# Expert rows gathered beside the layer work of the next token tile, with native fp32 products

## The chip, the cores and the metric

One core of one Trainium2 chip runs the whole program. The metric is device time in microseconds of one execution, lower is better.

## What is computed

A block with mLSTM, attention and a gated feed-forward part comes first. Then two layers of a second model follow, each over 256 tokens of width 1024 in float32. Layer 0 has a convolution and pooling mixer, layer 1 a sparse attention beside an HGRN recurrence; both then do cross attention to 256 memory tokens and a PEER feed-forward part. The reference, cut to what matters here:

```python
for l in range(2):
    hn = rmsnorm(h, mix_norm[l])
    h = h + (short_conv_pool_mixer(hn, ...) if l % 2 == 0 else sparse_attn_hgrn_mixer(hn, ...))
    h = h + memory_cross_attn(rmsnorm(h, xattn_norm[l]), mem_n, ...)
    h = h + peer_ffn(rmsnorm(h, peer_norm[l]), peer_wq[l], peer_keys[l], peer_u[l], peer_v[l])
return rmsnorm(h, final_norm)

# peer_ffn, for each token: 8 heads, two sets of 128 keys
s1, i1 = top_k(s[:, :, 0], 16); s2, i2 = top_k(s[:, :, 1], 16)
top, pos = top_k(s1[..., :, None] + s2[..., None, :], 16)      # of 256 candidates
eid = i1 * 128 + i2 at pos                                     # 128 experts of 16384 per token
act = gelu(einsum('td,ted->te', x, u[eid]))
out = einsum('te,ted->td', softmax(top) * act, v[eid])
```

## The kernel before

256 tokens are two tiles of 128 (NT = 2), one token a partition. The arrays uv0 and uv1 hold a row of u and one of v side by side, 8 KB per expert. For a tile and j = 0..127 (SEL), POOL issues one indirect DMA that fetches expert j of each of the 128 tokens: 1 MiB, called a row of the ring here. The ring has 9 slots (RING).

Each engine runs its own program in order and waits on semaphores; nothing but the code's order decides what comes first.

- Dense products use weight tiles of 1024 x 512 (2 MB, four parts; a ring of six parts, loaded by SP). Outside the memory keys and values of layer 1, ACT rounds each part to fp32r (`high`, L1136), POOL subtracts to get the rest (`low`, L579), and PE multiplies three pairs, hi x hi, lo x hi and hi x lo (`product`, L714), for all 256 tokens: tokens as moving operand in blocks of 256 (`transposed`) or weights as moving operand, 512 wide (`natural`).
- Layer work goes stage by stage for both tiles: `odd` (layer 1 only), then cross attention, then the queries. A list unit on DVE (`top_lists`, `candidates`, `top_heads`, `keys_of`) finds the experts of two heads of one tile; four make a tile's 128. They run for tile 0 before the gathers; for tile 1 in pieces between the dots of tile 0.
- The expert rows of a layer follow, 2 x 128. POOL waits for a slot (`rows_done`) and issues (L636). DVE makes the product with the token's activation, held in two PSUM banks (`dots`, L2027), four rows at a time (GROUP). ACT takes the gelu (L1185), DVE multiplies by the gate (L2037), ACT makes a diagonal matrix per row (L1191), and PE adds diagonal x v row to two banks (L800), two products of 512 columns a row. In layer 0, tile 0, PE also makes memory keys and values of layer 1 between the groups, in native float32 (`memory`).
- PSUM banks are handed out by a plan (`make_plan`) in the order of fills.

Of the kernel before, what the change touches and what calls it, by code (L numbers as in the profile page):

```python
# [32 lines left out]
P = 128  # L33
S = 256
# [25 lines left out]
RING = 9  # L60
GROUP = 4
GROUPS = SEL // GROUP
DIAGS = 8

# [99 lines left out]

def make_plan():
# [32 lines left out]
    for l in range(2):  # L198
        if l:
            p.add("T7", 4)  # L200

            p.add("o_ckv")
            p.add("o_ik")
            p.add("o_hf", 2, "scalar")
            p.add("o_hi", 2)
            p.add("o_hg", 2)
            p.add("o_hq", 2)
            p.add("o_iq", 2)
            p.add("o_ql", 4)
            p.add("o_cT")  # L210
            p.add("o_kT", 2)
            p.add("h_d0", 2, "scalar")
            for n, h in enumerate(LEVELS):
                if n + 1 < len(LEVELS):
                    p.add(f"h_d{n + 1}", 2, "scalar")
                p.add(f"h_s{n}", 1 if h == P else NT)
            p.add("h_diag", NT)
            p.add("h_pv", NT)
            p.add("idx", 8, "scalar")
            units_of(p, "o", 8)  # L220
            p.add("o_pv", 4)
            p.add("lat_T", 4)
            p.add("o_yc", NT)
            p.add("o_yT", 4)
            p.add("o_out", 4)
        p.add(f"T{5 + 3 * l}", 4)
        p.add(f"x_q{l}", 4)
        units_of(p, f"x{l}", 4)
        p.add(f"x_pv{l}", 4)
        p.add(f"x_oT{l}", 4)  # L230
        p.add(f"x_o{l}", 4)
        p.add(f"T{6 + 3 * l}", 4)

        for n in range(PH // 2):
            p.add(f"p_q{l}{n}", 2, taker="scalar")
            p.add(f"p_s{l}{n}")
            p.add(f"p_r{l}{n}", taker="scalar")
        p.add(f"p_h{l}", 2, marks=0, hold=True)
        for t in range(NT):
            p.add(f"p_v{l}{t}", 2, marks=0, hold=True)  # L240
            if l == 0 and t == 0:
                p.add("x_k1", 4)
                p.add("x_v1", 4)
            if t == NT - 1:
                p.release(f"p_h{l}")
            p.release(f"p_v{l}{t}")
# [3 lines left out]
def tiles_in_order():  # L250
# [9 lines left out]
    for l in range(2):  # L260
# [6 lines left out]
        if l == 0:  # L267
            t += [("x_k1", 1), ("x_k1", 3), ("x_v1", 1), ("x_v1", 3)]
# [8 lines left out]
def build(nc, io):  # L277
# [6 lines left out]
    with ExitStack() as ctx:  # L284
# [261 lines left out]
        def _(po):  # L546
# [93 lines left out]
            def low_cross(layer):  # L640
# [5 lines left out]
                if layer == 0:  # L646
                    load_gain(7)
# [1577 lines left out]
```

## Time and profile before

| what | value |
|---|---|
| median of 3 runs | 2677.15 us (2676.20 to 2685.51) |
| the profiled execution | 2676.58 us, span 2674.3 us |
| mean granted clock of PE | 0.909 |
| PE, DVE, POOL, ACT busy | 2111.0, 1453.6, 1141.1, 653.1 us |
| moved by DMA | 735.58 MB, mean 275 GB/s |

### The profile page before, as it was taken

The page shows a single profiled execution, that of the slowest core. Times are in us where ns is not written, and L with a number is a line of the kernel's source. Part 1 is how long each engine was busy: PE and PEld are TensorE (multiplying, and loading weights), DVE is VectorE, ACT ScalarE, POOL GpSimd, SP SyncE. Part 2 cuts the span into 40 slices and gives each one's busy share as a digit, 9 for nine tenths or more (in the row PEclk, how much of TensorE's full clock was granted, in tenths as well). Part 3 has the DMA queues.
Part 4 walks back from the last instruction along what each step waited for, and adds up shares of the span by engine and source line. Part 5 has one row for each costly group of instructions (what it writes and reads, how often), then busy time and mean ns, then how long its engine had stood idle before and what let it go on. Part 6 is the DMA issues. An engine that isn't in the chain of part 4 may idle for free. (4 is left out here: it accounts for less than half of the span.)

```text
span 2674.3 us, 23831 instructions
## 1 busy us (share of the span) xinstructions
PE 2111.0 (79%) x8566; PEld 1373.4 (51%) x8566; DVE 1453.6 (54%) x3135; ACT 653.1 (24%) x1247; POOL 1141.1 (43%) x809
## 2 busy tenths in 40 slices
PE   3899989999688498887778768858775887878776
PEld 3755679888577344333333337847672333333332
DVE  6353232147535977755555545672388776455554
ACT  1322333443233111111111124233331111111111
POOL 2612457797536333332333338214362333333332
PEclk7898989999898799999999989979898989989988
DMA  8455445565324599999999956113337999999996
GB/s 318 144 174 166 168 145 171 167 193 176 118 94 144 229 424 425 422 419 389 393 426 426 426 223 194 62 52 114 102 136 320 426 425 426 421 379 426 426 423 291
DMA packets 126934, 735.58 MB, mean 275 GB/s; under 512 B 14264, under 2 KB 14264, under 8 KB 60512
## 3 DMA queue, kind: packets, MB, share of 16 engines
q0 software_dynamic: 77600, 555.18, 49.9%
q1 hardware_dynamic: 49072, 178.83, 20.5%
q8 instruction: 68, 1.11, 0.2%
q14 instruction: 50, 0.41, 0.0%
q10 hardware_dynamic: 144, 0.05, 0.0%
HBM read 732.94 MB, written 1.06 MB: 274 GB/s over the span
## 5 line engine op out<-in xcount | busy, mean ns | idle before, releaser
L579 POOL TENSOR_TENSOR W_lo<-W,W_hi 128x1024 fp32r<-128x1024 f32 x264 | 642.6, 2442 | 423.7 <-ACT W_hi L1136 423.0
L800 PE MATMUL banks<-arena 128*128 128x512 f32 x912 | 449.5, 642 | 150.4 <-ACT arena L1191 150.4
L800 PE MATMUL banks<-rows_b,arena 128*128 128x512 f32 x684 | 341.1, 646 | 122.0 <-ACT arena L1191 122.0
L1136 ACT ACTIVATE W_hi<-W 128x1024 fp32r<-128x1024 f32 x264 | 277.4, 1058 | 471.3 <-PE banks L714 389.0
L800 PEld LDWEIGHTS banks<-arena 128*128 128x128 f32 x912 | 182.0, 204 | 405.3 <-issue 259.2
L2027 DVE SCALAR_TENSOR_TENSOR arena<-arena,banks 128x1024 f32<-128x1024 f32 x228 | 276.3, 1220 | 193.3 <-DMA arena<-in_uv,p_eid 192.1
L636 POOL DMA_INDIRECT arena<-in_uv,p_eid x228 | 214.8, 942 | 385.0 <-PE banks L800 376.4
L714 PE MATMUL banks<-HT_hi,W_hi 128*128 128x256 f32 x1128 | 327.2, 290 | 35.2 <-DVE HT_lo L1576 13.4
L714 PE MATMUL banks<-HT_hi,W_lo 128*128 128x256 f32 x1128 | 324.8, 288 | 0.0
L714 PE MATMUL banks<-HT_lo,W_hi 128*128 128x256 f32 x1128 | 324.6, 288 | 0.0
L800 PEld LDWEIGHTS banks<-rows_b,arena 128*128 128x128 f32 x684 | 138.7, 208 | 317.7 <-issue 206.9
L636 POOL DMA_INDIRECT rows_b<-in_uv,p_eid x171 | 160.6, 939 | 307.6 <-PE banks L800 295.9
L2027 DVE SCALAR_TENSOR_TENSOR rows_b<-rows_b,banks 128x1024 f32<-128x1024 f32 x171 | 207.6, 1220 | 153.8 <-DMA rows_b<-in_uv,p_eid 151.4
L1185 ACT ACTIVATE arena<-arena 128x4 f32<-128x4 f32 x128 | 26.3, 205 | 1050.8 <-DVE arena L2031 1050.8
L800 PE MATMUL banks<-rows_c,arena 128*128 128x512 f32 x452 | 219.3, 625 | 47.8 <-ACT arena L1191 47.8
L714 PEld LDWEIGHTS banks<-HT_hi,W_hi 128*128 128x128 f32 x1128 | 222.9, 198 | 38.1 <-DVE HT_lo L1576 13.5
L714 PEld LDWEIGHTS banks<-HT_hi,W_lo 128*128 128x128 f32 x1128 | 222.7, 197 | 0.0
L714 PEld LDWEIGHTS banks<-HT_lo,W_hi 128*128 128x128 f32 x1128 | 222.3, 197 | 0.0
L2027 DVE SCALAR_TENSOR_TENSOR rows_c<-rows_c,banks 128x1024 f32<-128x1024 f32 x113 | 137.2, 1220 | 100.0 <-DMA rows_c<-in_uv,p_eid 99.5
L714 PE MATMUL banks<-W_hi,HT_hi 128*128 128x512 f32 (+1 forms) x400 | 159.8, 400 | 36.9 <-issue 16.6
L636 POOL DMA_INDIRECT rows_c<-in_uv,p_eid x113 | 106.3, 941 | 162.1 <-PE banks L800 160.0
L800 PEld LDWEIGHTS banks<-rows_c,arena 128*128 128x128 f32 x452 | 87.6, 198 | 170.8 <-issue 102.1
(260 smaller groups left out, 2641.4 us busy)
## 6 DMA issues: line engine op xcount, KB each, us to landing
W<-in_weights SPq DMA_DIRECT2D x336, 512.0 KB, 3.6
gain<-in_rows POOLq DMA_DIRECT2D x10, 512.0 KB, 5.9
arena<-in_uv,p_eid POOLq DMA_INDIRECT x228
rows_b<-in_uv,p_eid POOLq DMA_INDIRECT x171
arena<-in_rows POOLq DMA_DIRECT2D x1, 2048.0 KB, 17.0
arena<-in_keys POOLq DMA_DIRECT2D x2, 1024.0 KB, 5.0
arena<-bias_scratch POOLq DMA_DIRECT2D x2, 1024.0 KB, 7.7
rows_c<-in_uv,p_eid POOLq DMA_INDIRECT x113, 10.9
```

The source lines that it names most:

```text
L579: po.tensor_tensor(W_lo[:, slot, :], W[:, (PARTS * n + part) % RAW_RING, :], W_hi[:, slot, :].bitcast(F32), ALU.subtract).then_inc(S_("lo_ ...
L636: po.indirect_dma_start(rows[slot], None, table, bass.IndirectOffsetOnAxis(ap=p_eid[:, t, j:j + 1], axis=0))\
L714: mm = pe.matmul(bank[:, out], x if stationary else y, y if stationary else x, start=start, stop=last)
L800: mm = pe.matmul(sums[c], diag[:, n % DIAGS, :], rows[slot][:, D + c * BLK:D + (c + 1) * BLK], start=j == 0, stop=j == SEL - 1)
L1136: act.activation(W_hi[:, q % SPLIT_RING, :], wait_landed(act, n, part), ACT.Copy).then_inc(S_("hi_made"), 1)
L1185: act.activation(a, a, ACT.Gelu_apprx_tanh).then_inc(S_("gelu_ready"), 1)
L2027: v.scalar_tensor_tensor(out=u, in0=u, scalar=1.0, in1=h, op0=ALU.mult, op1=ALU.mult, accum_out=p_act[:, t, j:j + 1]).then_inc(S_("row_dot ...
```

## The change

From the end of the even output on, the program is cut into four chains, (layer 0, tile 0), (layer 0, tile 1), (layer 1, tile 0), (layer 1, tile 1). A chain does one tile's layer work: `odd` if in layer 1, `cross`, `queries`. In chains 1 to 3, places (`feed`) are written into the code of DVE, ACT and PE; at each, the engine does its share of the next pair of rows (GROUP = 2) of the chain before. PE's place k does pair k - 2 (LAG). What is left of a chain's 64 pairs after its places is done at its end (`drain`). There are 39 places in `odd`, 15 in `cross`, 10 in `queries` and 16 in `memory`, which now follows the queries of chain 1. The last chain's rows are drained alone.

Dense products in the chains are native float32, 128 tokens at a time, straight from the parts that SP loads; ACT and POOL don't split them, and each weight tile of a layer is loaded once per token tile. POOL only issues gathers there. The dot's second operand is H in SBUF. The gelu is 0.5 a g (1 + tanh(...)): DVE makes two small products and a third, ACT a Tanh and one Identity a row. Gains, keys, masks and bias windows come from SP (`tables`), in its order among the weight parts, behind waits. The ring has 8 slots. The last norm, too, goes tile by tile.

```diff
-RING = 9
-GROUP = 4
+RING = 8
+GROUP = 2
+LAG = 2
...
+CHAINS = [(l, t) for l in range(2) for t in range(2)]
...
+            def tables(stage, i):
...
+                elif stage == "o_ik.3":
+                    load_masks(3)
...
+                elif i == 0 and stage in ("o_ql.2", "o_ql.3"):
+                    c = int(stage[-1])
+                    sp.wait_ge(S_("scratch_written"), 16)
+                    sp.wait_ge(S_("hscores_ready"), c - 1)
...
@@ PE
+            def weigh(g):
+
+                c = at[0]
+                for j in range(g * GROUP, (g + 1) * GROUP):
+                    n, slot, turn = row_of(c, j)
                     pe.wait_ge(S_("diag_ready"), n + 1)
...
+                    for b in range(2):
+                        mm = pe.matmul(banks[:, plan.bank(f"p_v{c}", b), :], diag[:, n % DIAGS, :],
+                                       rows[slot][:, D + b * BLK:D + (b + 1) * BLK], start=j == 0, stop=j == SEL - 1)
                     mm.then_inc(rows_done, 1)
...
+            def feed():
+
+                if at[0] is not None:
+                    if LAG <= at[1] < GROUPS + LAG:
+                        weigh(at[1] - LAG)
+                    at[1] += 1
+
+            def drain():
+
+                for g in range(max(at[1] - LAG, 0), GROUPS):
+                    weigh(g)
+                at[0] = None
+
+            def dense(stage, i, blocks):
+
+                n = tile_no[stage] + i
+                bank = claim(stage, i)
+                for part in range(PARTS):
+                    w = raw(n, part)
+                    for b, (out, columns, stationary) in enumerate(blocks):
+                        for j in range(2):
+                            x, y = w[:, j, columns], HT[:, 2 * part + j, :]
+                            mm = pe.matmul(bank[:, out], x if stationary else y, y if stationary else x,
...
+                    if part % 2:
+                        feed()
...
+            def queries(c, l, t):
+
+                turn_norm(c, 6 + 3 * l, t)
                 for n in range(PH // 2):
...
+                    dense(f"p_q{n}.{c}", 0, blocks4)
...
+            for c, (l, t) in enumerate(CHAINS):
+                if c:
+                    begin(c - 1)
+                if l:
+                    odd(c, t)
+                cross(c, l, t)
+                queries(c, l, t)
+                if c == 1:
+                    memory()
+                if c:
+                    drain()
+            begin(3)
+            drain()
...
@@ ACT
+            def row_weights(g):
+
+                c = at[0]
+                e = slice(g * GROUP, (g + 1) * GROUP)
+                act.wait_ge(S_("dots_ready"), c * GROUPS + g + 1)
+                step(act.activation(p_tanh[:, e], p_poly[:, e], ACT.Tanh, scale=0.7978845608028654))
                 for j in range(g * GROUP, (g + 1) * GROUP):
...
+                    step(act.activation(p_w[:, j:j + 1], p_tanh[:, j:j + 1], ACT.Identity, scale=p_half[:, j:j + 1],
+                                        bias=p_half[:, j:j + 1]))
...
@@ DVE
+            def dots(g):
...
+                    v.scalar_tensor_tensor(out=u, in0=u, scalar=1.0, in1=H[:, t, :], op0=ALU.mult, op1=ALU.mult,
+                                           accum_out=p_act[:, j:j + 1]).then_inc(S_("row_dots"), 1)
...
+                step.overlap(v.scalar_tensor_tensor(out=p_half[:, e], in0=a, scalar=0.5, in1=p_g[:, t, e], op0=ALU.mult,
+                                                    op1=ALU.mult))
+                stt(p_poly[:, e], a, 0.044715, a, ALU.mult, ALU.mult)
+                stt(p_poly[:, e], p_poly[:, e], 1.0, a, ALU.add, ALU.mult, "dots_ready")
...
+            def queries(c, l, t):
+
+                norm1(c, 6 + 3 * l, t)
+                feed(4)
+                for n in range(PH // 2):
+                    after(v, f"p_s{n}.{c}")
+                    top_lists(l, n)
+                    if n < PH // 2 - 1:
+                        feed()
+                    candidates(l, 2 * n, 2 * n + 2)
+                    top_heads(l, 2 * n, 2 * n + 2)
+                    keys_of(l, t, 2 * n, 2 * n + 2)
+                    if n < PH // 2 - 1:
+                        feed()
+                if c == 1:
+                    feed(16)
```

How the order moves on PE, at the output product of the cross attention of layer 1. Before (L788 sums with the values, L733 transposes, L714 the three products of the split operands, which then repeat):

```order
L1074 MATMUL banks<-x_kT,arena 128x256 x4
L778 MATMUL banks<-const,arena 128x128 x12
L788 MATMUL banks<-arena 128x256 x16
L733 MATMUL banks<-const,H 128x128 x16
L714 MATMUL banks<-W_hi,HT_hi 128x512
L714 MATMUL banks<-W_lo,HT_hi 128x512
L714 MATMUL banks<-W_hi,HT_lo 128x512
```

The same place of chain 2 in the change (L846 is `weigh`, L878 `dense`, L893 the transposes):

```order
L1206 MATMUL banks<-arena 128x256 x8
L846 MATMUL banks<-rows_b,arena 128x512 x4
L893 MATMUL banks<-const,H 128x128 x8
L846 MATMUL banks<-rows_c,arena 128x512 x4
L878 MATMUL banks<-W,arena 128x512 x4
L846 MATMUL banks<-arena 128x512 x4
L878 MATMUL banks<-W,arena 128x512 x4
L846 MATMUL banks<-arena 128x512 x2
L846 MATMUL banks<-rows_b,arena 128x512 x2
```

The dense work of one tile is native, and four products of the rows before stand after every half weight tile and every hand-over.

On DVE, at a list unit. Before, tile 0 (L2052 takes the scores, L1953 to L1971 make the lists, L1408 the candidates, then the heads):

```order
L2052 COPY arena<-banks 128x512
L1953 MAX arena<-arena 128x8 x4
L1955 MAX_INDEX p_idx<-arena 128x8 x4
L1957 MATCH_REPLACE arena<-arena 128x128 x4
L1959 MAX arena<-arena 128x8 x4
L1961 MAX_INDEX p_idx<-arena 128x8 x4
L1971 CAST arena<-p_idx 128x64
L1408 TENSOR_TENSOR arena<-arena 128x512
L1953 MAX arena<-arena 128x8 x2
```

In chain 1 of the change (L2098 is the dot, L2103 and L1672 the small products behind it):

```order
L2284 MAX arena<-arena 128x8 x4
L2286 MAX_INDEX p_idx<-arena 128x8 x4
L2288 MATCH_REPLACE arena<-arena 128x128 x4
L2290 MAX arena<-arena 128x8 x4
L2292 MAX_INDEX p_idx<-arena 128x8 x4
L2300 CAST arena<-p_idx 128x64
L2098 SCALAR_TENSOR_TENSOR rows_c,arena<-rows_c,H 128x1024 x2
L2103 SCALAR_TENSOR_TENSOR arena<-arena 128x2
L1672 SCALAR_TENSOR_TENSOR arena<-arena 128x2 x2
L1666 TENSOR_TENSOR arena<-arena 128x512
L2284 MAX arena<-arena 128x8 x2
```

The copy of the scores is gone (ACT takes them), and a pair of dots stands between the lists and the candidates.

## Rows read from the trace of the kernel before

**Rows 1.** The page, 40 slices: DMA engines busy in tenths, and GB/s.
```profile
DMA  8455445565324599999999956113337999999996
GB/s 318 144 174 166 168 145 171 167 193 176 118 94 144 229 424 425 422 419 389 393 426 426 426 223 194 62 52 114 102 136 320 426 425 426 421 379 426 426 423 291
```

**Rows 2.** Stages: us; busy of PE, PEld, DVE, ACT, POOL; PEclk, DMA share, GB/s.
```profile
0.00:732.10 732.10, 617.95 (x3356) 514.04 (x3356) 311.41 (x455) 242.78 (x291) 406.10 (x183) 0.91 0.54 176
732.10:816.00 83.90, 69.21 (x400) 61.06 (x400) 27.00 (x50) 32.07 (x49) 38.57 (x17) 0.94 0.36 113
816.00:915.00 99.00, 59.64 (x464) 58.27 (x464) 76.98 (x267) 27.13 (x36) 44.35 (x26) 0.80 0.53 187
915.00:1582.00 667.00, 540.31 (x1216) 238.57 (x1216) 394.89 (x898) 101.42 (x328) 232.61 (x248) 0.94 0.96 401
1582.00:1838.40 256.40, 193.97 (x1242) 176.15 (x1242) 145.54 (x247) 89.53 (x132) 105.37 (x49) 0.89 0.32 102
1838.40:1922.10 83.70, 68.96 (x400) 60.91 (x400) 27.00 (x50) 30.79 (x48) 38.61 (x18) 0.94 0.36 113
1922.10:2020.50 98.40, 59.56 (x464) 58.18 (x464) 77.20 (x266) 27.13 (x36) 43.41 (x25) 0.80 0.41 151
2020.50:2653.70 633.20, 494.26 (x1008) 203.26 (x1008) 387.05 (x884) 98.44 (x321) 232.03 (x247) 0.91 0.98 409
2653.70:2674.30 20.60, 7.13 (x16) 2.96 (x16) 6.50 (x22) 3.78 (x9) 0.00 (x0) 0.77 0.13 51
```

**Rows 3.** DVE in the gathers, timeline: start, us, engine, line, operation [idle before <-releaser].
```profile
1385.19 0.16 DVE L2037 TENSOR_TENSOR arena<-arena 128x4 f32<-128x4 f32 x1 [0.27 <-ACT arena L1185]
...
1388.35 1.22 DVE L2027 SCALAR_TENSOR_TENSOR arena<-arena,banks 128x1024 f32<-128x1024 f32 x1 [1.20 <-DMA arena<-in_uv,p_eid]
```

**Rows 4.** Timelines of PE and its weight loads: list scores, memory part, expert rows.
```profile
842.35 2.02 PE L1097 MATMUL banks<-arena 128*128 128x128 f32 x16 [0.79 <-issue]
...
1021.45 3.62 PE L714 MATMUL banks<-arena,W 128*128 128x256 f32 x16
...
1409.26 0.19 PEld L800 LDWEIGHTS banks<-rows_b,arena 128*128 128x128 f32 x1 [0.24 <-issue]
```

**Rows 5.** Timeline of ACT: the four diagonals of a group.
```profile
1414.79 1.28 ACT L1191 ACTIVATE arena<-const,arena 128x128 f32<-128x128 f32 x4 [0.23 <-DVE arena L2037]
```

**Rows 6.** Timeline of DVE: first tile's halves of the even output.
```profile
719.12 0.69 DVE L1526 TENSOR_TENSOR X<-banks,X 128x512 f32<-128x512 f32 x1 [12.74 <-PE banks L714]
...
730.00 0.69 DVE L1526 TENSOR_TENSOR X<-banks,X 128x512 f32<-128x512 f32 x1 [8.83 <-PE banks L714]
```

**Rows 7.** Timeline of DVE: a list with POOL splitting, and one (910.18) without.
```profile
865.26 0.69 DVE L2052 COPY arena<-banks 128x512 f32<-128x512 f32 x1
...
877.45 3.49 DVE L1998 TENSOR_TENSOR arena<-arena 128x512 f32<-128x512 f32 x2
...
882.83 0.69 DVE L2052 COPY arena<-banks 128x512 f32<-128x512 f32 x1
...
910.18 1.29 DVE L1998 TENSOR_TENSOR arena<-arena 128x512 f32<-128x512 f32 x2
```

**Rows 8.** Timeline of the last norm, ACT and DVE.
```profile
2662.04 1.06 ACT L1154 ACTIVATE H<-X 128x1024 f32<-128x1024 f32 x1 [6.34 <-PE banks L800]
...
2664.90 0.17 DVE L1411 TENSOR_SCALAR st<-st 128x2 f32<-128x2 f32 x1 [1.38 <-ACT H L1154]
...
2667.27 2.60 DVE L1414 SCALAR_TENSOR_TENSOR H<-X,st,gain 128x1024 f32<-128x1024 f32 x2
```

**Rows 9.** Timeline of DVE: an HGRN level's products (three such) and masked scores.
```profile
1716.97 1.22 DVE L1408 TENSOR_TENSOR arena<-arena 128x1024 f32<-128x1024 f32 x1
1718.23 1.29 DVE L1893 TENSOR_TENSOR arena<-banks,arena 128x512 f32<-128x512 f32 x2
```

**Rows 10.** Stage table as in group 2: gathers, memory tiles, lists together.
```profile
936.00:1137.00 201.00, 176.43 (x453) 86.98 (x451) 145.29 (x392) 28.18 (x95) 73.02 (x78) 0.97 1.01 424
```

**Rows 11.** Gather issues on POOL, line 636: duration ns min/median/max, first and last start.
```profile
L636 POOL DMA_INDIRECT arena<-in_uv,p_eid x228: 932/936/1389, 885.4 to 2630.7; - x114
```

More of the change, by code:

```diff
@@ L197, in make_plan @@
     p.add("e_out", 4)
[L198 to L246, printed above, removed]
+    for c, (l, t) in enumerate(CHAINS):
+        chain(p, c, l, t)
+        if c:
+            p.release(f"p_v{c - 1}")
+        p.add(f"p_v{c}", 2, marks=0, hold=True)
+    p.release("p_v3")
     return p
@@ new lines, in _ @@
+            for c, (l, t) in enumerate(CHAINS):
+                if c:
+                    at[:] = [c - 1, 0]
+                if l:
+                    odd(c, t)
+                cross(c, l, t)
+                queries(c, l, t)
+                if c == 1:
+                    memory()
+                act.wait_ge(S_("top_ready"), c + 1)
+                step(act.activation(p_g[:, t, :], p_g[:, t, :], ACT.Exp), "top_exp")
+                if c:
+                    drain()
+            at[:] = [3, 0]
@@ L1403, in _ @@
+            after(act, "p_v2", 1)
+            squares(0)
+            drain()
+            after(act, "p_v3", 1)
+            squares(1)
         @block.vector
@@ new lines, in feed, with drain @@
+            def feed(n=1):
+                for _ in range(n):
+                    if at[0] is not None and at[1] < GROUPS:
+                        dots(at[1])
+                        at[1] += 1
+            def drain():
+                c = at[0]
+                l, t = CHAINS[c]
+                for g in range(at[1], GROUPS):
+                    dots(g)
+                at[0] = None
+                v.wait_ge(rows_done, (c + 1) * SEL)
+                for b in range(2):
+                    xs = X[:, t, b * BLK:(b + 1) * BLK]
+                    step.free(v.tensor_tensor(xs, banks[:, plan.bank(f"p_v{c}", b), :], xs, ALU.add), f"p_v{c}", b)
@@ L2101, in _ @@
-            norm(10, X, gain_of(10), signal="final_ready")
+            for c, (l, t) in enumerate(CHAINS):
+                if c:
+                    at[:] = [c - 1, 0]
+                if l:
+                    odd(c, t)
+                cross(c, l, t)
+                queries(c, l, t)
+                softmax_top(c, t)
+                if c:
+                    drain()
+            at[:] = [3, 0]
+            norm1(3, 10, 0, "final_ready")
+            drain()
+            norm1(3, 10, 1, "final_ready")
```

1219 lines of the change are left out of this document (675 added, 544 removed).

## The prediction

> **What bounds the kernel now.** I read the slices of the span first, to find which resource is full where [rows 1]: the DMA engines stand at 9 tenths or more in two stretches, about 15 slices, and at 1 to 6 tenths over most of the rest. The stage table [rows 2] names them. From 915 to 1582 us and from 2020.5 to 2653.7 us the expert rows of a layer come in, 256 rows of 1 MiB, at 401 and 409 GB/s; the layers' other stages move 102 to 187 GB/s while PE is busy 69 of 84 us, 60 of 99, 194 of 256. So the kernel alternates: 1300 us bound by the gathers, 621 us of layer work (84 + 99 + 256 + 84 + 98) in which DMA mostly idles, and 732 us of front that the change leaves alone. In the gathers, DVE waits 1.20 us for each row beside 1.22 us of work [rows 3]. By bytes a row costs 1.05 MB / 426 GB/s = 2.46 us, a weight tile of 2.1 MB costs 4.92 us.
>
> **The change, part by part.** The program becomes four chains (layer, token tile); the rows of one chain are handled inside the next one's work, a pair per place. Prices of a place:
> - *DMA*: a pair is 4.92 us; there are 64 a chain.
> - *PE*: a row is 4 records of 0.43 us (a load of 0.19 and 0.24 of idle) [rows 4], so a pair is 3.44 us.
> - *DVE*: two products of 1.22 and three small operations of 0.16 with their waits, 3.1 us [rows 3].
> - *ACT*: before, four diagonals take 1.28 us [rows 5]; two of them, a Tanh and two small Identity are about 1.5 us. Never the bound.
>
> *Native fp32.* Before, a weight tile serves 256 tokens in 10.9 us (the second halves of the even output land at 719.12 and 730.00) [rows 6]. Native with 512 columns it is 16 records of 0.43 = 6.9 us for 128 tokens. With 128 columns it is 64 records; 16 of them take 2.02 us [rows 4], which would be 8.1, but a quarter of 0.43 is 0.108, and the row's last end is modelled, so 7 us. Two token tiles now cost 14 instead of 10.9. Their weights are read twice, 26 tiles x 4.92 = 128 us of DMA more, inside idle DMA time if the interleaving works. The splitting on ACT and POOL goes. That matters to DVE: its two 512-wide products of the key lookup take 3.49 us beside POOL's subtractions and 1.29 us where POOL only issues gathers [rows 7].
>
> *Chain 0* (no rows beside it). Cross attention: 4 tiles = 28 us, and for one tile instead of two the remaining 39 of the 84 us shrink to some 29 (a norm is 1.06 on ACT, 2.4 for the root and 1.3 for the product on DVE [rows 8], and halving the tokens doesn't halve the hand-overs): 57. Queries: norm, transposes and first tile 18 us, then four lists on DVE. One list took 17.6 us (from 865.26 to 882.83) [rows 7]; less the 2.2 of the stall, the copy of 0.7 that goes to ACT and some small stalls it is 14.2, so 57; with the softmax 78. Together 135, against 183 now (84 + 99).
>
> *Cross with rows* (15 places). PE: 15 x 3.44 + 28 + 12 for transposes, scores and sums = 92. DMA: 15 x 4.92 + 4 x 4.92 = 94. These are nearly equal, and the start (norm, first place without a pair, as PE lags by two) is exposed: 108.
>
> *Queries with rows* (10 places). DVE is the bound: 27 us to the first list, then 3 x (14.2 + 2 x 3.1) + 14.2 = 75, softmax 2: 105. DMA would need 69, so 36 us of it are lost in each of three chains.
>
> *Memory keys and values* (chain 1). PE 16 x (3.4 + 3.44) = 110: 16 records of 256 columns in 3.62 us are one such part [rows 4]. DMA needs 98. I take 114.
>
> *Rest of chain 1's rows*: 64 - 15 - 10 - 16 = 23 places at the pace of DMA, 113. With 6 us of hand-over (last sums, add) chain 1 is 108 + 105 + 114 + 113 + 6 = 446.
>
> *Odd mixer* (39 places, 10 weight tiles, one smaller). PE: 134 + 66 + 33 = 233. DMA: 39 x 4.92 + 49 + 10 for tables (a table of 1 MiB is 2.46) = 251. The HGRN levels are paced by DVE: half of 3 x 1.22 + 1.29 and 3.1, with waits about 5.9 a level [rows 9], 8 us over DMA in all. With start and hand-overs 272 for the first tile, 282 for the second, whose keys are twice as many. SP now waits for events of the chain before it loads masks and bias windows, and the weights of the next tiles queue behind those waits (the latent queries' behind the HGRN scores); PE has its sums and the index scores to do meanwhile, so I cost it at 0, and at 5 us, two such tables, if that cover is too short. Chain 2 = 272 + 108 + 105 + 4 = 489, chain 3 = 499.
>
> *End*: 128 rows with 8 already there, 120 x 2.46 = 295, and 17 for the last pair, norm of one tile instead of two and half the output (20.6 now [rows 2]): 312.
>
> Sum: 732 + 135 + 446 + 489 + 499 + 312 = 2613 us of span. The profiled execution takes 2676.58 for a span of 2674.3, and the median is 0.6 above it, so **2615 us**, 62 less. Put differently, hiding 1300 us of gathers under layer work saves much less than that work lasts, because PE has 220 us of row work per chain and most layer work is PE's too.
>
> Why not much worse: one stretch of before already does this. From 936 to 1137 us rows, memory tiles and list pieces run together at 424 GB/s, PE 176 of 201 us busy at a granted clock of 0.97 [rows 10].
>
> A page speaks against the DMA terms. The trace holds 426 GB/s for slices on end [rows 1]. The Trainium skill (SBUF — State Buffer, Summary: rules for kernel authors) says to estimate HBM to SBUF with 358 GB/s; by it a row would cost 2.9 us and the last drain alone 351. The row decides.
>
> **The rivals.**
> 1. *Near the DMA floor.* If places hide hand-overs entirely, and lists run while 8 rows buffer, chains 1 to 3 cost their bytes: 374 + 413 + 418 and the queries' 36 each, with 25 for starts: 732 + 135 + 1338 + 312 = 2517. For: [rows 10]. Against: 8 slots hold 20 us, and lists leave longer gaps.
> 2. *Slower: the clock in the chains.* PE is in program order behind DVE and ACT at every place. Where it pauses, the granted clock falls: 0.80 in the query stages (busy 60%), 0.89 in the odd mixer (76%), 0.94 in cross (82%) [rows 2]. PE at 0.8 would need 291 for the odd mixer, 115 for cross, 138 for memory; with the 39, 16 and 4 us of idle that I allow kept beside it, that is 330, 131, 142: 2 x 58 + 3 x 23 + 28 = 213 more, 2828. These stages hold 2 x 233 + 3 x 92 + 110 = 852 us of PE at full clock, so the gain of 62 is gone at 852 / (852 + 62) = 0.93. For: hand-overs at 64 places. Against: the places fill just those pauses with PE work, DMA sets the pace in half of them and hides a slower PE there, and [rows 10] have 0.97.
>    The Trainium skill (TensorE: Matmul & The Clock Gate, HAM oscillation — how this bites in real kernels) describes bursts between waits that keep finding a slow clock; the rows on the query stages agree with it.
> 3. *The dots fight for a port.* The dot's second operand moves from the banks to H in SBUF, so both come from SBUF. An issue on POOL is 0.936 us at the median and 1.389 at most [rows 11]. If each dot waited one issue, a pair on DVE would be 5.0 us: lists 3 x 11, levels 2 x 15, other places 20, and 64 x 0.1 in each drain: 90 more, 2705. Bounds: 0 (the median issue is as short as the shortest, though DVE often works on two SBUF operands beside it) to 0.94.
>    The Trainium skill (SBUF — State Buffer, Who interferes with whom) states that a DVE instruction with two SBUF inputs contends with a GpSimd instruction that reads SBUF; by it this rival holds, as far as issuing reads the indices. The before trace has no such dot.
> 4. *Nothing in sum*: interleaving gains and native fp32's extra 3.1 us for 26 tiles (80 us) cancel: 2664 to 2690.
>
> **How the numbers follow.** Forecast (2560 to 2664): 0.50. Rival 1: 0.15. Rival 2: 0.19. Rival 3: 0.04. Rival 4: 0.12. A measurement tells 0.5%, 13 us, from no change; below 2664 is faster: 0.50 + 0.15 = 0.65; same 0.12; slower 0.19 + 0.04 = 0.23. The range takes rival 1 in and reaches into rival 2: 2515 to 2735. The forecast's own is 2560 to 2664.
>
> **What would show it.** First row issue near 820 us and first dots near 867. DMA at 0.9 or more in cross and odd stages, 0.6 to 0.7 in queries; the queries of chains 1 to 3 about 105 us with DVE over 80% busy; PE's clock there at 0.8, elsewhere at 0.95 or more; four dense tiles at 7 us each net. A final drain of 2.46 us a row. Wrong if: the dots last over 1.3 us (rival 3); PE's clock in the odd mixer is below 0.93 (rival 2); odd plus cross of one chain last over 420 us at full clock, which would mean ordering waits that I have not seen, a take on ACT stuck behind a pair that hasn't landed.

## The result and the profile after

The changed kernel takes 2557.74 us (median of 4 runs, 2555.51 to 2559.21) against 2680.7 us (4 runs, 2676.2 to 2685.51): a ratio of 0.954, 95% interval 0.9518 to 0.9562. It is 123 us faster where 62 were forecast. That is inside the range of 2515 to 2735, but 2 us below the band of the forecast's own theory (2560 to 2664), on the side of rival 1. The profiled execution has a span of 2555.4 us.

The page, 40 slices of some 64 us. They answer to the slices of before [rows 1]:

```profile
PE   3898979999688498798779999985999998587776
PEclk7999989998889698899989999997999999799999
DMA  8455445565336599699999999986999999399997
GB/s 321 146 173 186 140 165 165 173 189 182 124 132 230 202 418 410 248 382 424 425 364 422 400 424 409 404 337 253 421 399 405 418 402 414 141 407 425 425 425 298
```

Before, the DMA engines were full in two blocks, with some 440 us of little traffic between them. Now they are at 9 from the 18th slice on, but for the 27th and 28th (the queries of chain 2), the 35th (the end of those of chain 3) and the last. The stage table, cut at DVE's adds to X (and, at 861.0, where chain 0's lists are done), shows the same (us; busy of PE, PEld, DVE, ACT, POOL; PEclk, DMA share, GB/s; it answers to [rows 2]):

```profile
0.00:727.10 727.10, 610.56 (x3356) 508.24 (x3356) 311.26 (x455) 240.63 (x289) 402.39 (x181) 0.92 0.54 177
727.10:782.10 55.00, 43.81 (x216) 32.60 (x216) 8.04 (x24) 8.32 (x17) 0.00 (x0) 0.91 0.45 157
782.10:861.00 78.90, 38.63 (x296) 37.12 (x296) 59.93 (x260) 8.58 (x15) 7.96 (x8) 0.76 0.61 224
861.00:955.70 94.70, 87.55 (x324) 52.44 (x325) 49.94 (x126) 30.70 (x89) 27.60 (x26) 0.93 0.84 340
955.70:1289.60 333.90, 279.98 (x893) 151.24 (x891) 199.95 (x602) 93.90 (x269) 113.70 (x102) 0.95 0.94 380
1289.60:1539.90 250.30, 230.29 (x923) 134.29 (x924) 167.76 (x413) 90.94 (x252) 78.67 (x75) 0.97 0.98 402
1539.90:1642.20 102.30, 94.06 (x336) 54.85 (x335) 50.74 (x129) 32.84 (x94) 32.63 (x30) 0.93 0.99 403
1642.20:1754.70 112.50, 80.82 (x390) 54.33 (x388) 88.86 (x329) 24.34 (x66) 24.47 (x24) 0.88 0.78 309
1754.70:2008.10 253.40, 237.95 (x963) 142.94 (x963) 165.71 (x407) 92.85 (x251) 81.68 (x74) 0.97 0.98 397
2008.10:2109.00 100.90, 92.02 (x333) 53.52 (x332) 50.61 (x129) 32.66 (x93) 31.34 (x29) 0.95 1.00 407
2109.00:2221.80 112.80, 82.25 (x392) 55.15 (x390) 88.85 (x330) 24.20 (x66) 26.39 (x25) 0.88 0.77 307
2221.80:2547.50 325.70, 241.31 (x512) 94.53 (x512) 187.38 (x463) 108.06 (x323) 138.99 (x120) 0.97 0.93 388
```

In order the rows are front, cross attention and queries of chain 0, cross attention of chain 1, its queries with memory tiles and drain, then odd mixer, cross attention and queries of chain 2 and of chain 3, and the last drain. Three readings lead the rest. In the odd mixers and the cross attentions of chains 2 and 3 the DMA engines are 0.98 to 1.00 busy. In the queries they are at 0.77, and nothing else is full either: DVE 89 of 113 us, PE 82. And the last drain takes 325.7 us at a share of 0.93, though it has nothing to do but rows.

The forecast against the stages, in us:

| stage | forecast | measured | difference |
|---|---|---|---|
| front | 732 | 727.1 | -5 |
| chain 0: cross, queries | 57, 78 | 55.0, 78.9 | -1 |
| chain 1: cross | 108 | 94.7 | -13 |
| chain 1: queries, memory, drain | 338 | 333.9 | -4 |
| chain 2: odd mixer | 272 | 250.3 | -22 |
| chain 2: cross, queries | 108, 109 | 102.3, 112.5 | -2 |
| chain 3: odd mixer | 282 | 253.4 | -29 |
| chain 3: cross, queries | 108, 109 | 100.9, 112.8 | -3 |
| end | 312 | 333.6 | +22 |

### The profile page after: what moved, and what is told of

Its sections match the earlier page's. It is cut to its first block, busy times and chain, and to the rows that moved or that the text cites. A ratio compares the mean times of both kernels' runs of the same rounds, so it can differ in the third digit from the quotient of the medians.

```text
span 2555.4 us, 26072 instructions
## 1 busy us (share of the span) xinstructions
PE 2119.2 (83%) x8926; PEld 1371.3 (54%) x8926; DVE 1432.2 (56%) x3674; ACT 789.2 (31%) x1821; POOL 965.8 (38%) x693
## 4 chain that ended last, share of the span: by engine, by line
PE 48%; DVE 24%; DMA 19%; ACT 5%; issue 3%; POOL 1%; DVEq 0%; SPq 0%; ACTq 0%; POOLq 0%
PE banks L846 16%; PE banks L758 14%; DMA rows_b<-in_uv,p_eid 13%; PE banks L878 9%; DMA rows_c<-in_uv,p_eid 4%; DVE arena L1666 3%; PE banks L1028 2%; DVE rows_b L2098 2%; PE banks L915 2%; DVE arena L1672 2%; DMA W<-in_weights 2%; ACT arena L1333 1%; DVE rows_c L2098 1%; DVE arena L2098 1%; DVE arena L2288 1%
## 5 line engine op out<-in xcount | busy, mean ns | idle before, releaser
L714 POOL DMA_INDIRECT arena<-in_uv,p_eid x192 | 213.1, 1110 | 669.8 <-PE banks L846 557.9
L667 POOL TENSOR_TENSOR W_lo<-W,W_hi 128x1024 fp32r<-128x1024 f32 x160 | 392.8, 2461 | 189.4 <-ACT W_hi L1280 188.9
L846 PE MATMUL banks<-arena 128*128 128x512 f32 x768 | 362.5, 610 | 85.6 <-ACT arena L1339 85.6
L846 PE MATMUL banks<-rows_b,arena 128*128 128x512 f32 x768 | 363.9, 612 | 26.6 <-ACT arena L1339 26.6
L2098 DVE SCALAR_TENSOR_TENSOR rows_b<-rows_b,H 128x1024 f32<-128x1024 f32 x192 | 233.7, 1224 | 197.6 <-DMA rows_b<-in_uv,p_eid 196.6
L2098 DVE SCALAR_TENSOR_TENSOR arena<-arena,H 128x1024 f32<-128x1024 f32 x192 | 233.9, 1225 | 177.9 <-DMA arena<-in_uv,p_eid 175.7
L714 POOL DMA_INDIRECT rows_b<-in_uv,p_eid x192 | 209.6, 1092 | 324.2 <-PE banks L846 314.8
L846 PEld LDWEIGHTS banks<-arena 128*128 128x128 f32 x768 | 140.7, 193 | 260.2 <-issue 158.7
L878 PEld LDWEIGHTS banks<-arena,W 128*128 128x128 f32 x2080 | 254.0, 200 | 31.2 <-issue 18.2
L878 PE MATMUL banks<-arena,W 128*128 128x128 f32 x2080 | 257.8, 284 | 11.1 <-ACT arena L1361 6.5
L846 PE MATMUL banks<-rows_c,arena 128*128 128x512 f32 x512 | 235.4, 603 | 33.5 <-ACT arena L1339 33.5
L846 PEld LDWEIGHTS banks<-rows_b,arena 128*128 128x128 f32 x768 | 147.9, 198 | 211.5 <-issue 167.8
L714 POOL DMA_INDIRECT rows_c<-in_uv,p_eid x128 | 140.7, 1099 | 248.3 <-PE banks L846 244.6
L2098 DVE SCALAR_TENSOR_TENSOR rows_c<-rows_c,H 128x1024 f32<-128x1024 f32 x128 | 155.3, 1225 | 118.3 <-DMA rows_c<-in_uv,p_eid 117.4
L1333 ACT ACTIVATE arena<-arena 128x1 f32<-128x1 f32 x512 | 197.9, 387 | 17.4
L758 PE MATMUL banks<-HT_hi,W_hi 128*128 128x256 f32 x608 | 177.2, 291 | 22.9 <-DVE HT_lo L1834 13.4
L1339 ACT ACTIVATE arena<-const,arena 128x128 f32<-128x128 f32 x512 | 177.6, 394 | 8.3
L846 PEld LDWEIGHTS banks<-rows_c,arena 128*128 128x128 f32 x512 | 94.9, 192 | 152.3 <-issue 99.4
L758 PE MATMUL banks<-HT_hi,W_lo 128*128 128x256 f32 x608 | 176.2, 290 | 0.0
```

The lines of the kernel that those rows point to most:

```text
L667: po.tensor_tensor(W_lo[:, slot, :], W[:, (PARTS * n + part) % RAW_RING, :], W_hi[:, slot, :].bitcast(F32), ALU.subtract).then_inc(S_("lo_ ...
L714: po.indirect_dma_start(rows[slot], None, io[f"uv{l}"], bass.IndirectOffsetOnAxis(ap=p_eid[:, t, j:j + 1], axis=0))\
L758: mm = pe.matmul(bank[:, out], x if stationary else y, y if stationary else x, start=start, stop=last)
L846: mm = pe.matmul(banks[:, plan.bank(f"p_v{c}", b), :], diag[:, n % DIAGS, :], rows[slot][:, D + b * BLK:D + (b + 1) * BLK], start=j == 0, ...
L878: mm = pe.matmul(bank[:, out], x if stationary else y, y if stationary else x, start=part + b + j == 0, stop=part == PARTS - 1 and b == le ...
L1333: step(act.activation(p_w[:, j:j + 1], p_tanh[:, j:j + 1], ACT.Identity, scale=p_half[:, j:j + 1], bias=p_half[:, j:j + 1]))
```

## The experiments

All runs are edits of the changed kernel. e1, e4, e8, e9 and e10 ran once; the others are medians of 4 or 6 runs, and their ratios are to the kernel before on the same chip, whose median lay between 2682 and 2685 us there. A few us of a total come from the front, which no edit touches: in the profiled executions it took 727.1 to 732.0 us. A stage that an edit leaves alone differs by up to 4 us from one execution to another.

### What the overlap is worth: e1_no_places

```diff
             def feed():
-                if at[0] is not None:
-                    if LAG <= at[1] < GROUPS + LAG:
-                        weigh(at[1] - LAG)
-                    at[1] += 1
+                pass
```

(the same for ACT's and DVE's `feed`.)

> Every place in the layer code is empty on PE, ACT and DVE, so all 128 rows of a chain are handled in its drain, and nothing of the native fp32 products or of the tile-by-tile order changes. Theory A (the gain is the overlap; native fp32 and one token tile at a time cost time by themselves): front 727, chain 0 133, chain 1 57 + 78 + 55 of memory tiles + 120 x 2.46 + 6 = 491, chains 2 and 3 some 150 + 57 + 78 + 301 = 586 each, end 334: 2857 us of span, between 2780 and 2900. Rival B (the gain comes from dropping the splits and the stalls of DVE beside POOL, the places add little): 2600 to 2700, near the kernel before.

Measured: 2847.49 us, span 2845.7. Chain 2 without rows, and its drain:

```profile
1339.00:1468.70 129.70, 108.86 (x621) 84.00 (x621) 57.13 (x141) 29.09 (x59) 0.00 (x0) 0.88 0.55 196
1468.70:1523.70 55.00, 43.32 (x216) 32.11 (x216) 8.00 (x23) 8.18 (x18) 0.00 (x0) 0.91 0.53 181
1523.70:1602.00 78.30, 36.77 (x296) 35.44 (x296) 59.76 (x258) 7.43 (x13) 0.00 (x0) 0.76 0.26 82
1602.00:1921.90 319.90, 239.08 (x512) 93.55 (x512) 183.63 (x450) 106.92 (x321) 148.40 (x128) 0.98 1.01 424
```

Theory A holds: 583 us for chain 2 where it said 586. So the change is a loss of 171 us (2845.7 against 2674.3) and a gain of 290 (2845.7 against 2555.4). The loss sits where a token tile costs more than half of two: two cross attentions of 55 against 84, two lots of queries of 78 against 99 [rows 2], about 2 x (26 + 57) = 166 over both layers. In the queries this is mostly overlap that the kernel before had and e1 lacks: its 99 us hold the lists of tile 0 only, and those of tile 1 ran between the dots. The odd mixer costs 129.7 and 137.2 for two tiles against 256.4 before, 10 us more. That native fp32 and dropping the splits are by themselves the gain is refuted. What native fp32 costs apart from the order by token tile, no run separates.

### What sets the pace beside the rows: e4, e9, e10

```diff
-                    for b in range(2):
+                    for b in range(2 if j in (0, SEL - 1) else 1):
```

> PE leaves out the second half of the v sum for all rows of a chain but the first and the last: a pair costs PE 1.72 us and not 3.44. Theory A (DMA sets the pace of the odd mixer, of cross attention and of the drains, DVE that of the queries): no stage gets shorter by more than 5 us but the cross attention of chain 1; 2530 to 2557. Rival B (PE in program order sets the pace of the odd mixer): 39 x 1.72 = 67 us less in each odd mixer and up to 26 in each cross attention, 2350 to 2450.

Measured: 2548.78 us, span 2547.0, 8 less, and inside theory A's band. The odd mixer and cross attention of chain 2:

```profile
1282.00:1536.50 254.50, 190.31 (x775) 118.89 (x775) 167.70 (x413) 90.33 (x252) 84.24 (x76) 0.87 0.96 391
1536.50:1634.80 98.30, 72.90 (x276) 43.42 (x276) 50.75 (x129) 32.56 (x94) 32.03 (x30) 0.86 1.01 417
```

PE is busy 40 us less and its granted clock drops from 0.97 to 0.87, yet the odd mixer is no shorter (254.5 against 250.3). PE's time there, at either clock, was not what was paid for. The 8 us came from chain 1's queries, memory tiles and drain, 325.9 us where 333.9 stood; the cross attention of chain 1, which theory A let get shorter, did not (see the hand-overs below).

e9 takes bytes away instead. It leaves out three quarters of each weight part in chains 2 and 3:

```diff
+                width = PW // 4 if tiles[n][0][-2:] in (".2", ".3") else PW
-                sp.dma_start(W[:, m % RAW_RING, :], io["weights"][weight_no[n]][:, part * PW:(part + 1) * PW])\
+                sp.dma_start(W[:, m % RAW_RING, 0:width],
+                             io["weights"][weight_no[n]][:, part * PW:part * PW + width])\
```

> In chains 2 and 3 only the first quarter of each weight part is loaded, the products then read what the slot held before: 3.7 us of transfer less for each tile, 37 us in an odd mixer and 15 in a cross attention, with all of PE's work left. Theory A (DMA sets the pace there, and PE, 230 of 250 us busy, is close behind): PE takes over, an odd mixer gets 8 to 15 us shorter, a cross attention 4 to 8, the queries don't change: 2515 to 2535. Rival B (DMA's 0.98 is a coincidence, the order of the hand-overs sets the pace): no stage changes by more than 3 us, 2552 to 2560. Rival C (DMA alone counts, PE has room): 2 x (37 + 15) = 104 less, 2454.

> The thin weights of e9 and the half v sum of e4 together: PE's 1.72 us a row pair less as well, in all chains. Theory A (two limits that lie close together in the odd mixer, DMA at 251 and PE at 233 by the forecast): each alone gives little, both together much: an odd mixer goes to 214 to 228 us, a cross attention to 80 to 88, 2465 to 2500 in all, more than the sum of what e4 (9 us) and e9 give. Rival B (hand-overs): the sum of e4 and e9, no more.

Measured: e9 2510.94 us (span 2507.7), e10 2445.92 us (span 2444.1). Odd mixer and cross attention of chain 2, first of e9:

```profile
1290.00:1525.70 235.70, 222.71 (x912) 131.92 (x913) 167.03 (x414) 91.85 (x252) 82.11 (x72) 0.98 0.94 361
1525.70:1616.50 90.80, 89.70 (x339) 51.78 (x338) 50.81 (x129) 32.55 (x94) 34.46 (x30) 1.00 1.00 389
```

and of e10:

```profile
1274.00:1491.60 217.60, 177.29 (x775) 112.12 (x775) 167.38 (x413) 90.69 (x252) 83.00 (x76) 0.91 0.98 397
1491.60:1579.80 88.20, 70.38 (x276) 42.76 (x276) 50.53 (x128) 32.65 (x94) 32.51 (x30) 0.88 0.99 396
```

With fewer bytes (e9) the odd mixer loses 15 us and PE is 94% busy; the cross attention loses 11.5 and PE is 99% busy. With both edits the odd mixer goes to 217.6. The spans fall by 8 and 48 us apart and by 111 together, twice the sum. Two limits lie close together, DMA first and PE 15 us behind. Both edits keep every hand-over and the number of transfers. e9 came out 4 us under theory A's band, since a cross attention gave 10 to 12 us where it said 4 to 8; rival C (PE has room) and the hand-over rivals are refuted. These are single executions, but the effects on the stages, 10 us and more, are well over the 4 us of spread.

### How far PE may lag: e3 and e8

```diff
-LAG = 2
+LAG = 1
```

(e8: `LAG = 3`.)

> LAG = 1: PE adds a pair one place behind DVE and ACT. Theory A (odd mixer and cross attention are at the DMA engines' limit, 0.98 to 1.00 busy, so PE's hand-overs are hidden, and what an earlier sum gives is only that the first slots of a chain come free one place sooner): 0 to 15 us less, 2543 to 2558. Rival B (a lag of one makes PE wait for ACT's diagonals, 1 to 2 us, at most of the 39 + 15 + 10 places): 2600 or more, with PE idle before the row products for ACT, and a lower clock in the odd mixer.

> LAG = 3: PE adds a pair three places behind DVE and ACT, so 6 of the 8 slots hold rows that are already multiplied, and 2 are left in flight. Theory A (what matters of the lag is how many slots it leaves to the transfers; a row lands some 5 to 8 us after its issue, and DVE waits for it in front of layer work that PE waits for): the HGRN levels and other hand-overs get 3 to 6 us longer at each of some 20 places in an odd mixer and 6 in a cross attention: 2620 to 2750 us, DMA well under 0.98 in the odd mixer; the last drain is unchanged at 324 us. Rival B (a longer lag only takes PE off the wait for ACT): 2550 to 2560.

Measured: e3 2556.97 us (4 runs), ratio 0.9524 [0.9498, 0.955]; e8 2651.73 us, span 2648.3. Chain 2 of e3, odd mixer, cross attention, queries:

```profile
1295.30:1542.50 247.20, 230.32 (x920) 134.27 (x921) 166.93 (x413) 93.06 (x254) 78.53 (x74) 0.97 0.99 407
1542.50:1640.00 97.50, 90.53 (x339) 51.91 (x338) 50.85 (x129) 31.86 (x91) 35.78 (x30) 1.00 1.02 421
1640.00:1757.40 117.40, 84.17 (x390) 54.16 (x388) 88.68 (x329) 24.37 (x66) 26.35 (x24) 0.86 0.76 297
```

and of e8, with the last drain:

```profile
1302.30:1575.60 273.30, 235.63 (x917) 139.91 (x917) 167.65 (x413) 90.50 (x252) 80.04 (x74) 0.93 0.94 370
1575.60:1690.40 114.80, 96.20 (x336) 55.87 (x336) 50.75 (x129) 32.44 (x94) 31.18 (x30) 0.91 0.90 360
1690.40:1809.10 118.70, 83.98 (x392) 57.65 (x392) 88.77 (x329) 24.01 (x66) 26.39 (x24) 0.85 0.75 288
2316.00:2640.40 324.40, 239.09 (x512) 93.74 (x512) 187.35 (x463) 108.08 (x323) 138.75 (x120) 0.97 0.93 390
```

Against the table of the changed kernel, a lag of one gives 3 and 5 us in the odd mixer and cross attention and gives 5 back in the queries, all near the spread of a stage; the total, 2556.97, is unchanged and in theory A's band (2543 to 2558). I had not expected that loss. It is DVE's wait for the scores of the first list, in the changed kernel and in e3:

```profile
1669.92 0.88 DVE L2284 MAX8 arena<-arena 128x8 f32<-128x128 f32 x4 [4.13 <-ACT arena L1361]
1672.82 0.87 DVE L2284 MAX8 arena<-arena 128x8 f32<-128x128 f32 x4 [8.98 <-ACT arena L1361]
```

ACT's copy of the first query tile ahead of it waits 7.06 us for PE's dense products in e3 and 3.68 in the changed kernel. A lag of three costs 23, 12 and 6 us in one chain and nothing in the drain, which has no places; 2651.73 us is in theory A's band (2620 to 2750), and rival B said 2550 to 2560. DMA's share falls from 0.98 to 0.94 in the odd mixer, and DVE's longest wait for a row there grows from 2.5 to 5.8 us. That fits theory A, that the lag has to leave slots for transfers: 4 of 8 are enough, 2 are not. The number of slots was not changed by itself.

### The queries: e2_take_first

In the trace of the changed kernel DVE waits 2.4 us or more in front of the search of each of the four key lists of a chain with rows. ACT, ahead of list 3 in chain 3 (start, us, engine, line, operation, [idle before <-releaser]):

```profile
2202.05 0.20 ACT L1331 ACTIVATE arena<-arena 128x2 f32<-128x2 f32 x1 [9.77 <-DVE arena L1672]
2202.28 0.81 ACT L1333 ACTIVATE arena<-arena 128x1 f32<-128x1 f32 x2
2203.12 0.69 ACT L1339 ACTIVATE arena<-const,arena 128x128 f32<-128x128 f32 x2
2203.72 0.57 ACT L1361 ACTIVATE arena<-banks 128x512 f32<-128x512 f32 x1
```

and DVE, for which that last copy is the scores to search:

```profile
2204.39 0.90 DVE L2284 MAX8 arena<-arena 128x8 f32<-128x128 f32 x4 [2.44 <-ACT arena L1361]
```

PE had the scores ready, but ACT takes them behind its share of the pair, which DVE has only just multiplied. The edit swaps the two:

```diff
                     take(p_qT[l], f"p_q{n}.{c}")
-                    feed()
                     if n:
                         act.wait_ge(S_("lists_ready"), (PH // 2) * c + n)
                     take(p_s[l], f"p_s{n}.{c}")
+                    feed()
```

> ACT copies the key scores of list n before it works on the pair of that place, not behind it. Theory A (DVE sets the pace of the queries, and each of lists 1 to 3 waits 2.44 us for this copy): 3 x 2.44 less in three chains, 22 us, so about 2536 us and a ratio of 0.945 to 0.947; the queries of chains 2 and 3 take 105 us and no longer 113. Rival B (the queries wait for transfers or for PE, DVE's wait only moves): 2553 to 2560, as without the edit.

Measured: 2533.66 us, ratio 0.9445 [0.9418, 0.9472]. The queries of chain 2:

```profile
1636.10:1741.20 105.10, 79.55 (x390) 52.91 (x388) 88.71 (x330) 24.74 (x66) 27.17 (x25) 0.93 0.84 332
```

105.1 us where 112.5 stood, with DVE's work unchanged at 88.7, and the wait in front of lists 1 to 3 is gone. Theory A holds, with 24 us where it said 22 (the ratio is just under its 0.945 to 0.947); rival B said no change.

### The ends of chains: e5, e6, e7

```diff
             at[:] = [3, 0]
+            feed(8)
             norm1(3, 10, 0, "final_ready")
             drain()
```

(ACT likewise, ahead of `squares(0)`.)

> The last norm of token tile 0 comes after 8 pairs of the last drain, not ahead of them. Theory A (from the last list to the first new row issue DMA is empty, and DVE's norm of 4.9 us lies on that path; later in the drain DVE waits 2 us a pair and hides it): 5 us less, about 2553 us, ratio 0.951 to 0.953; the last drain from the add of chain 2 to that of chain 3 takes 319 us and no longer 324. Rival B (the first issues wait for something else, such as PE's sums or POOL): no change, 2556 to 2559.

Measured: 2553.37 us (6 runs), ratio 0.9524 [0.9497, 0.9551]. By the total alone 4 us are at the edge of what is told apart. By the stage they are plain: from the add at 2223.53 to that at 2544.22 us is 320.7 against 325.7. The empty stretch at the head of the drain, in the changed kernel on POOL:

```profile
2210.35 0.94 POOL L714 DMA_INDIRECT rows_c<-in_uv,p_eid  x1 [1.79 <-PE banks L846]
2235.35 0.94 POOL L714 DMA_INDIRECT arena<-in_uv,p_eid  x1 [24.07 <-PE banks L846]
```

and in e5:

```profile
2212.07 0.94 POOL L714 DMA_INDIRECT rows_c<-in_uv,p_eid  x1 [1.76 <-PE banks L846]
2231.99 0.94 POOL L714 DMA_INDIRECT arena<-in_uv,p_eid  x1 [18.99 <-PE banks L846]
```

In the changed kernel no row is asked for during 25.0 us: all 8 slots are taken, POOL waits until PE frees one, and PE until DVE has finished list 3, the softmax and the norm and has multiplied a pair. Without the norm it is 19.9 us.

e6 moves two places of the odd mixer into that stretch:

```diff
-                dense(f"o_hi.{c}", 0, wide)
+                dense(f"o_hi.{c}", 0, wide, places=False)
...
                     top_lists(l, n)
-                    if n < PH // 2 - 1:
-                        feed()
+                    feed()
...
                     keys_of(l, t, 2 * n, 2 * n + 2)
-                    if n < PH // 2 - 1:
-                        feed()
+                    feed()
```

(PE and ACT each get two places behind the loop over the lists, and ACT and DVE one `feed(2)` fewer beside o_hi; `places=False` leaves out the two of that product.)

> Two places of the odd mixer (beside its product o_hi) move behind the last list of the queries, in each chain with rows. Theory A (the odd mixer and the drain of chain 1 are at DMA's limit, 4.92 us a place; DVE sets the pace of the queries, 2.87 us a place, and DMA idles at their end): 3 x 2 x (4.92 - 2.87) = 12 us less, 2545 us, the queries 6 us longer and the odd mixers 10 us shorter. Rival B (PE or the hand-overs set the pace of the odd mixer, so that fewer places there give nothing): 17 us more, 2570 to 2580.

> The edits of e2, e5 and e6 together. Theory A (they act at three different places of the path): 24 + 5 + 12 = 41 us less, 2511 to 2523 us, ratio 0.937 to 0.941. Rival B (with e2 the queries are no longer DVE's alone, and the places moved there meet PE or DMA): 2525 to 2540.

Measured: e6 2563.98 us, ratio 0.9565 [0.9529, 0.96], 6 us slower; e7 2540.15 us, ratio 0.9475 [0.944, 0.9509], slower than e2 alone (2533.66). e6's 2563.98 fits neither of its theories; e7's is at the upper edge of rival B's band (2525 to 2540). The intervals of the ratios overlap those of the runs they are compared with, and 5 of e6's 6 us could be the front, which took 732.0 us in its profiled execution against 727.1. From the front's end to the last add e6 takes 1824.0 us against 1820.3. What is sure is that the 12 us that theory A promised did not come. Half of A came true: e6's odd mixers take 241.6 and 242.8 us, 9 and 11 less. But its queries take 126.1 and 123.4, 14 and 11 more and not 6. DVE's waits at the end of e6's chain 3 show why:

```profile
2225.36 0.29 DVE L2359 TENSOR_REDUCE st<-arena 128x8 f32<-128x128 f32 x1 [1.78 <-ACT arena L1652]
2230.05 1.42 DVE L2127 TENSOR_TENSOR X<-banks,X 128x512 f32<-128x512 f32 x2 [3.83 <-PE banks L846]
```

The last pair stands right before the end of the chain, so the softmax waits behind ACT's diagonals (0.50 before) and the add waits for PE's sum (no wait before). These two waits are 5.1 us more and the two pairs some 6, together the 11 of chain 3.

### The version that follows: e11 and e12

e11 is e2 and e5 together. e12 adds the places of e6, but puts the second one before `keys_of`, the last step of the last list unit, and not behind it:

```diff
                     top_heads(l, 2 * n, 2 * n + 2)
+                    if n == PH // 2 - 1:
+                        feed()
                     keys_of(l, t, 2 * n, 2 * n + 2)
```

> The edits of e2 and e5 together, without that of e6. Theory A (both lie on the path, at different places): 24 + 5 = 29 us less, 2525 to 2532 us, ratio 0.941 to 0.944. Rival B (one takes the other's place): 2533 or more.

> The edits of e11, and the two places that e6 moved, but the second one ahead of the last key list and not behind it. Theory A (what e6 paid over 5.7 us a chain is the softmax behind ACT's diagonals, 1.3 us, and the add behind PE's sum of the last pair, 3.8 us; with some 9 us of DVE work behind the pair both are hidden): 4 to 12 us less than e11, 2515 to 2524 us, and queries of 111 us in chains 2 and 3 where e7 had 116 to 118. Rival B (each place in the queries costs 5 to 6 us, wherever it stands): 2532 to 2542, as e7.

Measured: e11 2533.56 us (6 runs), ratio 0.9443 [0.9418, 0.9468]; e12 2522.14 us (6 runs), ratio 0.9399 [0.9374, 0.9423]. In e12 the same two operations read:

```profile
2188.03 0.29 DVE L2363 TENSOR_REDUCE st<-arena 128x8 f32<-128x128 f32 x1 [0.44 <-ACT arena L1652]
2188.91 1.42 DVE L2128 TENSOR_TENSOR X<-banks,X 128x512 f32<-128x512 f32 x2
```

At this place the second wait is gone and the first is 0.44 us (in chain 2 the add still waits 0.90). The queries take 113.1 and 110.9 us, and e12 is 11 us faster than e11: theory A. By its total, e11 falls into rival B's band (2533 or more) by 0.6 us, and its interval overlaps e2's. Its trace speaks for A: both edits do what they did alone (queries of 105.1 us, last drain 321.5), and from the front's end to the last add it takes 1791.3 us, the 29 less than 1820.3 that A said. e12 takes 1783.4. e12 is the fastest of the runs that leave nothing out, 36 us below the changed kernel.

## Why the prediction was right, and where it was off

**The mechanism** was right: the gathers run under layer work, DMA is full in odd mixer and cross attention, and drains run at the pace of rows. PE's sum for an odd mixer, 233 us, was measured at 230.3 and 238.0. The size of the gain was not: 123 us and not 62. Chains 1 to 3 came out 73 us under the forecast, front and chain 0 together 6 under, and the end 22 over it, so part of the error cancels in the 57 us by which the span is shorter.

DMA's sum, 251, was met by the stage itself, 250.3 and 253.4, but in part by luck. POOL issued 75 rows in the first odd mixer and not the 78 of 39 pairs, and the stage moved 402 GB/s x 250.3 us = 100.6 MB, which at 426 GB/s would take 236 us. Fewer bytes and a lower rate than assumed cancel.

**The terms that were too dear** are the hand-overs. The prediction put 21 us on top of DMA's 251 in the first odd mixer and 31 in the second ("with start and hand-overs 272 ... 282"), and 14 on top of 94 in each cross attention. Most of the missing gain lies there: 50 us came back in the two odd mixers, 26 in the three cross attentions. A stage that is at DMA's limit doesn't pay for its hand-overs as long as landed rows wait in slots, and the second tile's doubled keys are hidden as well. e4, e9 and e10 show this limit; e8 shows that two slots free for transfers are too few for it.

The cross attention of chain 1 is another case, and half of the 26 us are its. It consists of a start and a stretch at DMA's limit:

```profile
861.00:878.00 17.00, 9.97 (x45) 8.41 (x46) 13.80 (x39) 6.09 (x17) 0.00 (x0) 0.60 0.15 47
878.00:955.70 77.70, 77.58 (x280) 44.03 (x279) 36.14 (x87) 24.61 (x72) 27.60 (x26) 1.00 1.00 404
```

The start, 17 us in which all 8 slots are taken and none is free for an issue, was even longer than the 14 forecast. What was too dear is DMA's 94: 8 rows were there already, and POOL issued 26 in the stage and not 30. The stage moved 340 GB/s x 94.7 us = 32 MB, where 94 us at 426 GB/s are 40. In e4, with half of PE's row products gone, the two parts take 16.9 and 77.6 us.

**The queries** were sized well but for one wait: 105 and 4 forecast, 112.5 and 112.8 measured. The list of 14.2 us with 6.2 of pairs was right: the period is 22.4 us (from 2181.97 to 2204.39), of which 2.44 are ACT's late copy, and 20.0 are left. e2 took it away and got 105.1. The sentence "a take on ACT stuck behind a pair" stood among the signs, but for the odd mixer, where DMA set the pace; it should have been priced in the one stage where DVE sets the pace.

**The end** was 22 us too cheap. The rate was right: the issues from 2235.35 to 2526.5 us are 120 in 291.2, one every 2.45 us. But the first comes 13.5 us after the add, because 8 landed rows don't keep DMA busy, they block it until the first pair is summed; and from the last issue to the end 28.9 us pass, where I had 17.

**Native fp32** was right: 64 records of 128 columns take 7.31 us between 800.35 and 807.7, and in chain 0 two halves of an output follow each other in 6.87 us (the adds at 774.50 and 781.37). Front and chain 0 came within 6 us in all, and the ordering waits on SP show no cost: DMA is 0.98 busy in the stages that have them.

**The rivals.** Rival 1 (2517), which I gave a chance of 0.15, was nearer than my own forecast: chains 1 to 3 took 1361 us, where it had 1338 and I had 1434. Its main step, that places hide the hand-overs, is the one that the odd mixers bear out. The span was 38 us above its sum: 23 in the chains and 22 in the end, which it shares with my forecast, less the 6 of front and chain 0. Rival 2 fell: the granted clock is 0.97 in the odd mixers and 0.93 to 0.95 in the cross attentions, and e4, at 0.87, is no slower. In chain 0's queries, without rows, it is 0.76, near the 0.80 of before [rows 2]; with rows it is 0.88 in chains 2 and 3, and without them (e1, chain 2) 0.76 again. I had said 0.8 there and 0.95 or more elsewhere. Rival 4 (cancelling, 2664 to 2690) fell by the time itself, and e1 splits the sum: 290 gained against 171 lost.

Rival 3 fell as it was put, that a dot waits for an issue: all 512 dots from two SBUF operands take 1.218 to 1.296 us.

```profile
L2098 DVE SCALAR_TENSOR_TENSOR arena<-arena,H x192: 1218/1225/1246, 864.1 to 2526.7; 128x1024 f32<-128x1024 f32 x192
L2098 DVE SCALAR_TENSOR_TENSOR rows_b<-rows_b,H x192: 1218/1225/1259, 868.1 to 2534.1; 128x1024 f32<-128x1024 f32 x192
L2098 DVE SCALAR_TENSOR_TENSOR rows_c<-rows_c,H x128: 1218/1225/1296, 872.7 to 2539.0; 128x1024 f32<-128x1024 f32 x128
```

But there is contention, and the issue pays for it. An issue in the changed kernel that begins during a dot, and one in the kernel before, whose dot has its second operand in PSUM:

```profile
945.71 1.23 DVE L2098 SCALAR_TENSOR_TENSOR rows_b<-rows_b,H 128x1024 f32<-128x1024 f32 x1 [2.45 <-DMA rows_b<-in_uv,p_eid]
945.85 1.90 POOL L714 DMA_INDIRECT rows_c<-in_uv,p_eid  x1 [4.21 <-PE banks L846]
```

```profile
1393.23 1.22 DVE L2027 SCALAR_TENSOR_TENSOR arena<-arena,banks 128x1024 f32<-128x1024 f32 x1 [1.22 <-DMA arena<-in_uv,p_eid]
1393.25 0.94 POOL L636 DMA_INDIRECT rows_c<-in_uv,p_eid  x1 [0.78 <-PE banks L800]
```

In the changed kernel 187 of the 512 issues begin during a dot. 159 of them last over 1.0 us, up to 1.98, and end 0.80 to 0.83 us after that dot; the other 28 begin within its first 0.04 or its last 0.17 us. In the kernel before 208 begin during a dot, and each lasts 0.93 to 0.95 us. The Trainium skill (SBUF — State Buffer, Who interferes with whom) has such a pair contend, as far as issuing reads SBUF; this trace agrees, with up to 1.0 us more for an issue and none for the dot. The stretched issues add some 80 us to POOL's busy time. What this costs the kernel was not tried; in the last drain the issues still follow each other every 2.45 us at a DMA share of 1.00 (2235.35 to 2526.5 us).

## What to carry to other kernels

Add up each resource's own time in a stage before adding hand-overs: where one engine or queue is full and there are buffers in front of it, hand-overs and a lower clock elsewhere are free, and a cheaper second resource gives little until the first is relieved (e4 8 us, e9 48, both 111). In a stage whose pace is set by an engine in program order, look at what stands ahead of the copies it waits for, and put its input first and the side work second. Side work may fill a stretch, but not right before a hand-over: two places moved to the end of the queries lost time where the second stood behind the last list unit (e6, and e7 against e11, 7 us), and gained 11 us (e12 against e11) where it stood one step earlier, before `keys_of`.

## What the runs showed of the hardware

- The granted clock follows PE's work even where time does not change: with half the v products PE was busy 190 us and not 230 in an odd mixer of nearly the same length (254.5 and 250.3), and the clock went from 0.97 to 0.87.
- At a DMA share of 0.98 to 1.00 the odd mixers moved 397 to 402 GB/s and the cross attentions 403 to 407, against 424 at 1.01 in the drain of e1 with rows alone. Per unit of share that is 2 to 4% less. Weights beside rows are not the reason alone: with LAG = 1 the cross attention of chain 2 moved 421 at 1.02, and the kernel before has 424 at 1.01 with rows and memory tiles together [rows 10]. What it is was not tried.
- Where an indirect DMA issue on POOL began during a DVE product with both operands in SBUF, it ended some 0.8 us after that product and took up to 1.98 us (159 of 187 such issues). Beside a product with one operand in PSUM it stayed at 0.93 to 0.95 us (all 208). The product itself was not longer.
